# A decoder-block kernel: output banks swapped, a second convolution buffer, gate rows one slab later, one wait dropped

## The reference

```
h  = rmsnorm(x);  u = h @ w_in          # split: mq mk mv mo mi mf gq gk gv gr ga
qk = silu(causal_conv(concat(mq, mk)))  # width 4, per feature
mLSTM heads (4) on mq, mk, mv with gates mi, mf; gated by sigmoid(mo)
gated linear attention heads (4) on gq, gk, gv, decay from log_sigmoid(ga @ wa2 + ba)/16;
    gated by silu(gr)
x += concat(both) @ w_out
p  = softmax(rmsnorm(x) @ wq . keys);  x += (p . values) @ wo      # keys, values from 256 memory rows
x += square(relu(rmsnorm(x) @ w1)) @ w2
out = rmsnorm(x)
```

## Time and profile before

| | us |
|---|---|
| median of 3 runs | 3049.03 (3047.67 to 3050.71) |
| the profiled execution, device time | 3047.55 |
| its span in the trace | 3046.0 |
| TensorE matmuls busy | 2956.7 (97%) |
| VectorE busy | 1572.3 (52%) |
| ScalarE busy | 1261.8 (41%) |
| GpSimd busy | 336.2 (11%) |
| mean granted TensorE clock | 0.996 |

### The profile page before, as it was taken

One profiled execution on the slowest core, in us unless ns is written; L12 is line 12 of the kernel. 1 busy time (PEld: TensorE's weight loads), 2 busy tenths in 40 slices (PEclk: granted clock), 3 DMA queues, 4 the chain that ended last, 5 costly groups with the idle time before them and its releaser, 6 DMA issues.

```text
span 3046.0 us, 44503 instructions
## 1 busy us (share of the span) xinstructions
PE 2956.7 (97%) x15836; PEld 2427.7 (80%) x15836; DVE 1572.3 (52%) x2805; ACT 1261.8 (41%) x2474; POOL 336.2 (11%) x627
## 2 busy tenths in 40 slices
PE   6999999999999999999999999999999999999998
PEld 6877788888877787888877778788887778788886
DVE  5375654444466655443457564444446665544444
ACT  5554444333445344432345444433344533443233
POOL 2243100000033300000004310000002330000000
PEclk9999999999999999999999999999999999999999
DMA  5732122433342122333234212243334212233332
GB/s 176 249 97 63 56 90 83 133 96 96 93 138 90 56 79 88 125 92 101 90 109 135 68 53 92 87 132 94 93 96 139 91 57 77 83 98 97 97 97 76
DMA packets 150581, 301.73 MB, mean 99 GB/s; under 512 B 13809, under 2 KB 13937, under 8 KB 150385
## 3 DMA queue, kind: packets, MB, share of 16 engines
q1 hardware_dynamic: 139776, 262.38, 28.2%
q0 software_dynamic: 10176, 35.70, 3.1%
q10 hardware_dynamic: 432, 1.05, 0.1%
HBM read 282.27 MB, written 16.81 MB: 98 GB/s over the span
## 4 chain that ended last, share of the span: by engine, by line
PE 83%; ACT 6%; DVE 5%; issue 4%; DMA 1%; SPq 0%; ACTq 0%; DVEq 0%; POOL 0%; POOLq 0%
PE bank L1524 69%; PE work L1524 5%; ACT hr L996 2%; PE work L1538 2%; DVE qk L1260 1%; ACT w_hi L635 1%; DVE mw L1319 1%; PE work L1628 1%; PE bank L1575 1%; DVE w_lo L1058 1%; DMA vo_dram<-folded 1%; PE work L1666 1%; ACT mw L890 1%; ACT pr L792 1%; PE work L1691 1%
## 5 line engine op out<-in xcount | busy, mean ns | idle before, releaser
L1058 DVE TENSOR_TENSOR w_lo<-raw,w_hi 128x512 fp32r<-128x512 f32 x976 | 680.3, 701 | 1330.6 <-ACT w_hi L635 1330.4
L635 ACT ACTIVATE w_hi<-raw 128x512 fp32r<-128x512 f32 x976 | 611.0, 631 | 1466.8 <-PE bank L1524 1357.1
L1524 PE MATMUL bank<-act_hi,w_hi 128*128 128x512 f32 x1408 | 557.0, 396 | 1.0
L1524 PE MATMUL bank<-act_lo,w_hi 128*128 128x512 f32 x1408 | 549.7, 390 | 0.0
L1524 PE MATMUL bank<-act_hi,w_lo 128*128 128x512 f32 x1408 | 549.5, 390 | 0.0
L1524 PE MATMUL bank<-w_hi,h_hi 128*128 128x512 f32 x1152 | 454.1, 394 | 1.7 <-ACT hr L996 1.0
L1524 PE MATMUL bank<-w_lo,h_hi 128*128 128x512 f32 x1152 | 448.8, 390 | 0.0
L1524 PE MATMUL bank<-w_hi,h_lo 128*128 128x512 f32 x1152 | 448.8, 390 | 0.0
L1524 PE MATMUL bank<-w_hi,act_hi 128*128 128x512 f32 x768 | 312.5, 407 | 10.0 <-ACT zz L937 5.9
L1524 PEld LDWEIGHTS bank<-act_hi,w_hi 128*128 128x128 f32 x1408 | 265.1, 188 | 62.1 <-ACT hr L996 7.7
L1524 PEld LDWEIGHTS bank<-act_hi,w_lo 128*128 128x128 f32 x1408 | 265.1, 188 | 56.3
(11 more groups left out here) (280 smaller groups left out, 3634.6 us busy)
## 6 DMA issues: line engine op xcount, KB each, us to landing
raw<-in_w_dram SPq DMA_DIRECT2D x256, 512.0 KB, 3.7
raw<-in_w_in_dram SPq DMA_DIRECT2D x112, 512.0 KB, 3.6
raw<-in_w_out_dram SPq DMA_DIRECT2D x32, 512.0 KB, 3.8
raw<-kq_dram SPq DMA_DIRECT2D x32, 512.0 KB, 3.7
raw<-vo_dram SPq DMA_DIRECT2D x32, 512.0 KB, 3.7
xres<-in_x_dram POOLq DMA_DIRECT2D x16, 512.0 KB, 5.8
tok<-in_x_dram POOLq DMA_DIRECT2D x12, 512.0 KB, 7.8
out_dram<-xres POOLq DMA_DIRECT2D x12, 512.0 KB, 3.9
```

The costliest lines, as they stand in the source:

```text
L635: nc.scalar.activation(w_hi[:, slot, :], raw[:, pair_slot, slot % 2, :], ACT.Copy).then_inc(slab_hi, 1)
L1058: tt(w_lo[:, slot, :], raw[:, pair_slot, slot % 2, :], w_hi[:, slot, :].bitcast(F32), ALU.subtract).then_inc(slab_lo, 1)
L1524: ins = mm(dst, left, right, start=(kt == 0 and j == 0), stop=(kt == KT - 1 and j == 2))
```

## The change

- `gqk` and `gv` become one tensor `gqkv`; `ubuf` becomes a list of two views, the first in `zz` as before (mq), the second in `gqkv` (mk). The wait for `conv_done` before evicting mk is dropped.
- GpSimd's third chunk of distances waits for four convolutions instead of eight.
- The gate rows and what follows are asked one step later: TensorE L1736 and L1741 in step 3, L1748 in step 7, L1753 in step 9; ScalarE L840 in step 3, L846 and L849 in step 4, L855 to L860 in step 5; VectorE L1238, L1242 in step 4, L1272 to L1277 in step 5, L1282, L1284 in step 7, L1246 to L1249 in step 9. The decay scans L1301 to L1307 go from step 7 to step 6. ScalarE's L864 to L866 stay in step 9.
- TensorE no longer waits for `m_exp` before the key transposes.
- In step 54 ScalarE asks for the sigmoid table ahead of its tile evictions.
- The attention output goes to `bank` and then `wbank`, without waits for free banks; instead TensorE waits before the first block for four evicted probability tiles, before the second for eight. Probability tiles 4 to 7 go through `wbank`; norm tiles 0 to 3 of the MLP go through `bank`, and the MLP's first block waits for at least four of them.

```diff
-        ubuf = zz[:, 0:4 * (GROUP + 3)].rearrange("p (i n) -> p i n", i=4)
+        ubuf = [t[:, 0:4 * (GROUP + 3)].rearrange("p (i n) -> p i n", i=4) for t in (zz, gqkv)]
...
-                        pool.wait_ge(conv_done, KT * g + KT)
+                        pool.wait_ge(conv_done, KT * g + 4)
...
-                    if s == 2:
+                    if s == 3:
                         act.wait_ge(grow_full, g + 1)
...
-                    if s == 3:
+                    if s == 4:
                         act.wait_ge(grow_out, g + 1)
...
-                    if s == 4:
+                    if s == 5:
                         act.wait_ge(la_abs, g + 1)
...
                     if s == 54:
                         head_guess(1)
+                        nc.scalar.preload_act_table_set("sigmoid_and_others")
...
-                                if b == B_MK:
-                                    act.wait_ge(conv_done, KT * g + i + 1)
...
-                    if s == 3:
+                    if s == 4:
                         dve.wait_ge(grow_out, g + 1)
...
-                    if s == 8:
+                    if s == 9:
                         dve.wait_ge(mcol_full, g + 1)
...
-                    if s == 4:
+                    if s == 5:
                         dve.wait_ge(row_log, g + 1)
...
-                    if s == 6:
+                    if s == 7:
                         dve.wait_ge(mlast_full, g + 1)
...
-                    if s == 7:
+                    if s == 6:
                         dve.wait_ge(la_log, g + 1)
...
-                        add_block(U_O + 4 * b, b * COLS, (wbank, bank)[b])
+                        add_block(U_O + 4 * b, b * COLS, (bank, wbank)[b])
...
-                    if s == 2:
+                    if s == 3:
                         pe.wait_ge(gates_low, g + 1)
...
-                    if s == 6:
+                    if s == 7:
                         pe.wait_ge(row_scan, g + 1)
...
-                    if s == 8:
+                    if s == 9:
                         pe.wait_ge(mrow_ready, g + 1)
...
                         if stage == 1:
-                            pe.wait_ge(m_exp, 8 * g + 2 * c + 2)
...
+                    if r == 0:
+                        pe.wait_ge(act_lo_ready, TRS * g + PRO_TR + TR_PROBS + 4)
...
+                    if r == KT:
+                        pe.wait_ge(act_lo_ready, TRS * g + PRO_TR + TR_PROBS + KT)
                     block_slab(s, "token", U_O + 4 * b, TR_PROBS if b == 0 else None, pt_hi, pt_lo,
-                               (wbank, bank)[b], b == 0)
+                               (bank, wbank)[b], False)
...
-                            pe.wait_ge(act_lo_ready, TRS * g + PRO_TR + TR_NORM1 + kt + 1)
+                            pe.wait_ge(act_lo_ready, TRS * g + PRO_TR + TR_NORM1 + max(kt + 1, 4))
```

More of the change, by code:

```diff
@@ L152, in program @@
         mixing = ExitStack()
-        gqk = sb("gqk", [P, 4, GROUP], F32, mixing)
-        gv = sb("gv", [P, NCH, COLS], F32, mixing)
+        gqkv = sb("gqkv", [P, 2 * 4 * GROUP], F32, mixing)
+        gqk = gqkv[:, 0:4 * GROUP].rearrange("p (i n) -> p i n", i=4)
+        gv = gqkv[:, 4 * GROUP:].rearrange("p (c n) -> p c n", c=NCH)
         zz = sb("zz", [P, NCH * LEVELS * 256], F32, mixing)
         Z = zz[:, :].rearrange("p (b l n) -> p b l n", b=NCH, l=LEVELS)
-        ubuf = zz[:, 0:4 * (GROUP + 3)].rearrange("p (i n) -> p i n", i=4)
+        ubuf = [t[:, 0:4 * (GROUP + 3)].rearrange("p (i n) -> p i n", i=4) for t in (zz, gqkv)]
         zmin = zz[:, 4 * (GROUP + 3):4 * (GROUP + 3) + 2 * GROUP].rearrange("p (j n) -> p j n", j=2)
@@ L779, in norm_tile @@
                 def norm_tile(k, kt, into):
-                    tile_hi(TRS * g + PRO_TR + (TR_NORM0, TR_NORM1)[k] + kt, kt, GROUP, k + 1, into)
+                    tile_hi(TRS * g + PRO_TR + (TR_NORM0, TR_NORM1)[k] + kt, kt, GROUP, k + 1, into,
+                            bank if k and kt < 4 else wbank)
                 def probs_tile(kt):
-                    tile_hi(TRS * g + PRO_TR + TR_PROBS + kt, kt, GROUP, None, pt_hi, bank)
+                    tile_hi(TRS * g + PRO_TR + TR_PROBS + kt, kt, GROUP, None, pt_hi, bank if kt < 4 else wbank)
                 def prob_exps(b):
@@ L871, in group @@
                         read_out(act, g, k)
[L872 removed]
+                        nc.scalar.activation(qk[:, k, :], ubuf[b - 1][:, r // 2, CONV - 1:], ACT.Identity,
                                              scale=conv_w[:, CONV - 1, k:k + 1],
@@ L933, in group @@
                             if b in (B_MQ, B_MK):
-                                k = 4 * b + i
-                                if b == B_MK:
-                                    act.wait_ge(conv_done, KT * g + i + 1)
-                                nc.scalar.activation(ubuf[:, i, 3:], bank[i][:], ACT.Copy)\
+                                nc.scalar.activation(ubuf[b][:, i, 3:], bank[i][:], ACT.Copy)\
                                     .then_inc(bank_free, 1)
@@ L1144, in norm_tile @@
                 def norm_tile(k, kt, hi_lo):
-                    tile_lo(TRS * g + PRO_TR + (TR_NORM0, TR_NORM1)[k] + kt, kt, GROUP, k + 1, hi_lo)
+                    tile_lo(TRS * g + PRO_TR + (TR_NORM0, TR_NORM1)[k] + kt, kt, GROUP, k + 1, hi_lo,
+                            bank if k and kt < 4 else wbank)
                 def probs_tile(kt):
-                    tile_lo(TRS * g + PRO_TR + TR_PROBS + kt, kt, GROUP, None, (pt_hi, pt_lo), bank)
+                    tile_lo(TRS * g + PRO_TR + TR_PROBS + kt, kt, GROUP, None, (pt_hi, pt_lo),
+                            bank if kt < 4 else wbank)
                 def score_max(b):
@@ L1254, in group @@
                             read_out(dve, g, k)
-                            mark(nc.vector.tensor_copy(ubuf[:, i, 0:CONV - 1], halo[:, k, :]))
+                            mark(nc.vector.tensor_copy(ubuf[b - 1][:, i, 0:CONV - 1], halo[:, k, :]))
                             acc = qk[:, k, :]
@@ L1263, in group @@
                                     link(ins)
-                            nc.vector.tensor_copy(halo[:, k, :], ubuf[:, i, GROUP:]).then_inc(conv_done, 1)
+                            nc.vector.tensor_copy(halo[:, k, :], ubuf[b - 1][:, i, GROUP:]).then_inc(conv_done, 1)
                         else:
@@ L1824, in norm_tile @@
                     tiles_out(TRS * g + PRO_TR + (TR_NORM0, TR_NORM1)[k],
-                              {kt: [(bank_free, use_no(g, u + (4 if kt < 4 else 8)))]}, NCH, [kt], xres)
+                              {kt: [(bank_free, use_no(g, u + (4 if kt < 4 else 8)))]}, NCH, [kt], xres,
+                              bank if k and kt < 4 else wbank)
                 for s in range(B_OUT * KT, B_Q * KT):
@@ L1837, in turn_probs @@
                     pe.wait_ge(pr_ready, 8 * g + 4 * (kt // 4) + 4)
-                    tiles_out(TRS * g + PRO_TR + TR_PROBS, {}, NCH, [kt], pr_rows, bank)
+                    tiles_out(TRS * g + PRO_TR + TR_PROBS, {}, NCH, [kt], pr_rows, bank if kt < 4 else wbank)
                 for s in range(B_Q * KT, B_O * KT):
@@ L1872, in mlp_pass @@
                         slab(slab_no(g, B_MLP * KT + s, hb), kt, "feature" if b < 2 else "token",
-                             use_no(g, U_MLP + 4 * b - 4, hb),
+                             use_no(g, U_O, hb) if first and b == 0 else use_no(g, U_MLP + 4 * b - 4, hb),
                              act_hi if b < 2 else h_hi, act_lo if b < 2 else h_lo)
```

2 lines of the change are left out of this document (1 added, 1 removed).

## The result

| | before | after |
|---|---|---|
| median, us (6 runs each, side by side) | 3048.80 | 3033.55 (3032.37 to 3035.38) |
| ratio to before | | 0.995, 95% interval 0.9937 to 0.9963 |
| profiled execution / span | 3047.55 / 3046.0 | 3033.43 / 3031.9 |
| mean granted clock | 0.996 | 0.995 |

The change is faster by 15 us. The forecast was 3021, with 3032 as its upper end: the direction was right, but the forecast gain of 28 us is nearly twice the measured 15.

What follows compares the result with a forecast made beforehand. TensorE, busy for 97% of the span, was taken as the bound. Terms -24.8 - 10.9 - 3.4 + 10.4 + 6.8 - 6.0 = -27.9 gave 3019.7 us for the profiled execution, 3021 for the median; own range 3010 to 3032.

Steps and rivals of the forecast that it cites:

- The dropped wait: TensorE's wait at L1779 before the key transposes, 16 waits: all of it goes, -24.8 us, bounds 0 and -24.8.
- the gate wait: TensorE's wait before L1736 for gT: asking a slab later saves 4 x 2.72, -10.9 us, bounds -10.9 and -11.7.
- The chain behind the gate rows: Step 9: VectorE's four operations follow convolution 0, then wait for ScalarE's sigmoid; L1268 starts 2.8 us later.
- the slab-16 wait: TensorE's wait before slab 16, 1.46 us idle, ends 2.6 later each group: +10.4, bounds 0 and +14.8.
- The first rival: TensorE's wait before slab 16 does not grow; +10.4 and +6.8 fall away: 3004 us at the median, chance 0.22.
- what the move does behind it: Passage on VectorE, ScalarE and GpSimd after the gate rows' move, from the decay scans to slab 16: +10.4 us.
- The column product at L1755: TensorE's single-column product in step 9 may wait 0.4 us for the scan at L1284; the slab-16 wait absorbs it.
- Full block: Rival: GpSimd's 28 moved operations block VectorE, which becomes the bound of slabs 16 to 23: 3057 us, chance 0.07.
- Half clock: TensorE's throttled stretches: two after gate waits go, -3.4 us; one comes per group after slab 16's wait, +6.8.
- Attention: Attention output in other banks: first slab's waits go, 1.5 of 2.0 us stays gained: -6.0, bounds -4 and -8.
- The table load in step 54: Wait at L1391, 4.0 us, could go (-4.6) or grow by the load (+5.1); middle taken, 0.
- The relaxed GpSimd wait: Last two distance passes, 28 operations, run beside the second convolutions; fits with 0.06 us to spare: 0, +2 as bound.

Runs made afterwards that it cites:

- k6_drop: The kernel before without TensorE's wait on m_exp in the convolution loop, and nothing else: 3026.85 us, -21.9, ratio 0.9932.
- k2_hold: The changed kernel, with GpSimd waiting for VectorE's first product before its second distance pass: 3024.94 us, -25.1 to the kernel before, ratio 0.9917.
- k3_pause: The changed kernel, with GpSimd waiting for its own signal between levels of its second distance pass: 3022.29 us, -27.8 to the kernel before, ratio 0.9908.
- k5_gate: The kernel before with only the eleven step numbers of the gate chain changed as in the change: 3061.45 us, +12.7, ratio 1.0042.
- n9_evict: The changed kernel, with ScalarE evicting the block's four banks before the sigmoid in steps 15 and 23: 3017.44 us, -32.3 to the kernel before, ratio 0.989.
- n10_refit: The changed kernel, gate rows still asked later, but last-row transposes in step 7, column product, last-maximum copy and decay scans put back: 3013.42 us, ratio 0.988.
- n11_both: The changed kernel with the edits of n9_evict and n10_refit, without the table load in step 54: 2997.57 us, -52.2 to the kernel before, ratio 0.9825.
- k1_swap: The changed kernel, with ScalarE in step 9 doing the sigmoid before its three gate-row exponentials: 3015.49 us, -34.6 to the kernel before, ratio 0.9888.
- m6_attn: The kernel before with only the attention and norm tile banks and the second convolution buffer as in the change: 3041.00 us, -7.8, ratio 0.9979.

## Why the prediction was right and wrong

- **The dropped wait, -24.8, and the gate wait, -10.9:** right, by the trace of the change and by k6_drop (-23.9 and, in the change, -10.9). The room of 2.5 us before the next release was enough; what the forecast did not have is the short wait for the state behind it.
- **The chain behind the gate rows, as a mechanism:** right. VectorE's sleep was forecast at 2.8 and is 2.80 in four groups, released by the line named, and with the other fault out of the way (k2_hold) the slab-16 wait lasts 3.7 for a forecast of 4.1. The first rival, that it does not grow, falls.
- **The step that failed** is in the passage on what the move does behind it: "GpSimd, started 1.2 earlier, stops competing before the end; I take 0.2 off." I had moved GpSimd by its first pass only. Its second pass waits for the very `row_p` that I was moving, so it did not come earlier; it started inside VectorE's sleep and held out the first operation after it for 4.0 us. The term was forecast at -0.2 a group and was +4.0; with the product let in, the time is 3022 to 3025 (k3_pause, k2_hold), inside the range. It shows as the slab-13 row (+8.9), where I had written that the w_lo were three slabs ahead, and in the half clock behind slab 13. The slab-16 wait came out 3.9 under its term, mostly because in groups 2 and 3 TensorE came late to it from half clock (2.4 there, 3.9 and 3.7 in groups 1 and 4).
- **The column product at L1755, +2.0:** the wait of 0.4 was forecast. It has nothing to do with the held-out product, since k2_hold has the same row (1.4, 4 waits). That the slab-16 wait absorbs it fits k2_hold, where that wait is 0.4 short of the forecast.
- **The price of the conflict could not be read from the trace before.** The trace of the kernel before shows GpSimd paying (0.85 for 0.40), and VectorE arriving after an idle time in a running stream at little cost (0.86 at 940.16). So even with the second pass in its right place these rows would have given some 0.2 for what turned out as 4.0. "Full block" was quoted against one part of the change, the third distance pass, and was rated there at 0.07; it was never asked of the other places where the change makes the two meet.
- **Half clock:** forecast net +3.4, measured +6.8. After slab 16 it came in three of the four groups; the stretches behind slab 13, and the double length of one, were only inside the bound.
- **Attention, -6.0:** measured -5.7, and this close partly by luck. The first slab's waits were worth 2.5 a group instead of 2.0. The new wait is at the fourth slab and on the line named, and costs 1.0 instead of 0.5; the forecast's own times gave it 0.85 (1189.15 - 1188.3), of which it charged 0.5.
- **The table load in step 54, 0:** +0.6 by the slab-56 row, inside its bounds.
- **The relaxed GpSimd wait, 0 with +2 as a bound:** mis-sized; 6 where it decides, 0 where other waits cover it.
- **Range:** its upper end took in the bounds of two terms only, the slab-16 wait (+4.4) and the half clock (+6.8), and none for a term that it did not have. The bounds of the attention output (+2.0), the kept half clock (+3.4), the table load (+5.1) and the relaxed wait (+2) were left out. The change was 1.5 us above it.

## What to carry to other kernels

When a step moves, follow its signal to every engine that waits for it, the idle ones too: here the semaphore that made ScalarE late also chose the moment at which GpSimd began. And check a sum of waits against the starts of the same slab in both traces: by the rows alone the attention output gave 4.0 here instead of 5.7, and a sum can come out right by two such errors. Two edits that look like one (ask later; do the chain later) are worth separate forecasts: the first gave 11 us, the second took some 24 (12.7 + 10.9), and what matters of the chain could stay where it was. And a buffer that breaks a dependency gives nothing until the program's order uses it: 0 alone, 17 us with the evictions moved ahead of the sigmoid (6.8 of it by half clock).

## What the runs showed of the hardware

- A 128x512 VectorE product that became ready while GpSimd ran its 0.40 us operations back to back took 4.73 us, in each of the four groups, and 4.74 to 4.76 in those of k5_gate and n9_evict. With a break of 0.08 us in the stream it took 0.71 (k3_pause). The Trainium skill ("SBUF — State Buffer", section "Who interferes with whom") has whoever issues first hold the shared ports for the whole instruction while the other blocks. By that rule the product would have lost the rest of one instruction, at most 0.4; in the trace eleven more go ahead of it.
- Being held out this long is the exception. Of some 380 arrivals of a w_lo or a product after an idle time, with at least three more GpSimd operations following without a break, counted over all the traces, 14 were held for over 1 us: these twelve products and two w_lo of 2.51 (988.34 in n10_refit, 1695.97 in n11_both), whose stream was of GpSimd's multiplications. The others took at most 0.4 more than usual. What makes the difference stays open.
- It goes the other way too, though for a shorter time: beside three 128x512 VectorE operations without a break (894.83 to 896.70) one GpSimd operation took 2.33 us (k1_swap):

```profile
894.27 0.40 POOL L550 TENSOR_TENSOR zz<-decay 128x128 f32<-128x128 f32 x1
894.64 2.33 POOL L549 TENSOR_TENSOR zz<-decay 128x128 f32<-128x128 f32 x1
```

- Waits change more than their own length. The change, k2_hold, k3_pause and k5_gate, with waits of up to 3.4 to 3.9 us before slab 16, have 20.4 to 23.8 us at half clock in their groups; k1_swap, with up to 2.7 there, has 6.8; n10_refit, whose longest wait in a group is 1.8, and n11_both have none. Length alone does not tell: with gate waits of 2.2 to 3.1 in all four groups k6_drop has four stretches, the kernel before two and m6_attn one. What exactly decides was not tried.

What stays open: the table load of step 54 was never run alone. The row of slab 56 is 4.6 in the change and 4.0 in the kernels without the load, so it costs some 0.6 by that row. Nor was n9_evict tried with the old single buffer, where the evictions would have to wait for the fourth convolution.
